# The shared expert's down products moved into the last eight passes of a mixture-of-experts loop

## The reference

```python
    def body(acc, blk):
        tok_b, gate_b, eb = blk
        xb = x_pad[tok_b]
        hb = jax.nn.silu(xb @ w_gate[eb]) * (xb @ w_up[eb])
        yb = hb @ w_down[eb]
        return acc.at[tok_b].add((yb * gate_b[:, None]).astype(acc.dtype)), None
    ...
    shared = (jax.nn.silu(x2 @ w_sh_gate) * (x2 @ w_sh_up)) @ w_sh_down
    return acc[:T] + shared
...
    x = layer_norm(DEEPNORM_ALPHA * x + ffn, ln2_g[i], ln2_b[i])
```

## Time and profile before

| | us |
|---|---|
| median of 3 runs | 1978.24 |
| lowest and highest of them | 1967.44, 1980.79 |
| the profiled execution, whole | 1967.62 |
| its span, first to last instruction | 1965.9 |
| share of the span in which PE is busy | 91% |

### The profile page before, as it was taken

How to read it: one execution, slowest core, us unless ns; L and a number is a source line. 1 busy time by engine, 2 the same in 40 slices (tenths; PEclk the granted TensorE clock), 3 DMA queues, 4 the chain that set the end, 5 groups by cost and what they waited for, 6 DMA issues and landing times. The chain is left out here.

```text
span 1965.9 us, 36214 instructions
## 1 busy us (share of the span) xinstructions
PE 1794.3 (91%) x12636; PEld 1109.1 (56%) x12637; DVE 750.8 (38%) x2168; ACT 384.9 (20%) x882; POOL 354.9 (18%) x450
## 2 busy tenths in 40 slices
PE   9999989889999888879999979999889999997877
PEld 7888444456666555543444438855456666664442
DVE  4222754723332322224255553415623333332225
ACT  2112650111111111102255243211011111110001
POOL 8442000011111111110012712200111111111110
PEclk9999999999999999999999989899999999999999
DMA  6220215599999999999122220015899999999997
GB/s 223 80 84 23 97 59 237 210 397 421 421 421 422 422 422 421 422 421 361 57 65 76 65 42 3 29 60 245 327 408 415 422 421 421 420 421 421 422 415 309
DMA packets 144184, 541.80 MB, mean 276 GB/s; under 512 B 31030, under 2 KB 68498, under 8 KB 94302
## 3 DMA queue, kind: packets, MB, share of 16 engines
q1 hardware_dynamic: 122782, 490.20, 62.2%
q0 software_dynamic: 21312, 50.37, 6.6%
HBM read 521.58 MB, written 46.14 MB: 289 GB/s over the span
## 5 line engine op out<-in xcount | busy, mean ns | idle before, releaser
L718 PE MATMUL bank<-W,XT 128*64 128x256 f32 x2880 | 324.7, 381 | 33.6 <-DMA W<-in_w_exp_up_dram 17.7
L718 PEld LDWEIGHTS bank<-W,XT 128*64 128x64 f32 x2880 | 233.4, 137 | 135.1 <-DMA W<-in_w_exp_gate_dram 26.0
L755 PE MATMUL bank<-W,ht 128*64 128x512 f32 x720 | 166.1, 602 | 13.4 <-DMA W<-in_w_exp_down_dram 8.1
L2237 PE MATMUL bank<-XT,room 128*128 128x512 f32 x352 | 158.9, 606 | 0.0
L729 DVE TENSOR_TENSOR sig<-sig,bank 128x256 f32<-128x256 f32 x72 | 30.3, 421 | 263.7 <-ACT sig L725 263.7
L718 PE MATMUL bank<-room,XT 128*64 128x256 f32 x864 | 104.0, 393 | 17.0 <-DMA room<-in_w_exp_gate_dram 8.8
L731 DVE TENSOR_TENSOR h<-sig,bank 128x256 f32<-128x256 f32 x72 | 30.3, 421 | 218.1 <-PE bank L718 218.0
L2237 PEld LDWEIGHTS bank<-XT,room 128*128 128x128 f32 x352 | 66.3, 193 | 82.3 <-issue 82.1
L784 POOL DMA_INDIRECT y_rows<-y,row x36 | 36.6, 1018 | 418.3 <-DVE y L777 418.3
L784 POOL DMA_INDIRECT y_rows<-XT,row x36 | 36.3, 1008 | 414.5 <-DVE XT L777 414.5
L704 ACT ACTIVATE XT<-bank 128x512 f32<-128x512 f32 x74 | 44.2, 597 | 334.5 <-PE bank L696 334.5
(11 more groups left out here) (490 smaller groups left out, 2793.0 us busy)
## 6 DMA issues: line engine op xcount, KB each, us to landing
W<-in_w_exp_gate_dram SPq DMA_DIRECT2D x88, 1024.0 KB, 25.5
W<-in_w_exp_up_dram SPq DMA_DIRECT2D x88, 1024.0 KB, 27.4
W<-in_w_exp_down_dram SPq DMA_DIRECT2D x88, 1024.0 KB, 26.9
room<-in_w_exp_gate_dram SPq DMA_DIRECT2D x40, 1024.0 KB, 24.2
third_high<-in_w_exp_down_dram SPq DMA_DIRECT2D x40, 1024.0 KB, 25.7
W<-y_rows SPq DMA_DIRECT2D x24, 1024.0 KB, 13.4
third_up<-in_w_exp_up_dram SPq DMA_DIRECT2D x20, 1024.0 KB, 27.5
w_shg<-in_w_exp_up_dram SPq DMA_DIRECT2D x20, 1024.0 KB, 24.2
```

Of the source, the lines that this page charges most:

```text
L718: last = pe.matmul((gate, up)[m][64 * a:64 * a + 64, :], xt[s][:, k, 64 * a:64 * a + 64], weights(w, a, m)[:, k * FE:(k + 1) * FE], start= ...
L755: last = pe.matmul(B[5 + half][64 * a:64 * a + 64, :], ht[:, j, 64 * a:64 * a + 64], weights(w, a, 2)[:, at:at + 512], start=(j == 0), sto ...
L2237: last = pe.matmul(main(i)[:], wc[i % WBUFS][:, kb, :], K.XT[:, kb, :], start=(kb == 0), stop=(kb == KD - 1))
```

## The change

- The loop writes the last eight passes out as well, after the hardware loop, and gives each pair of them a tile: pass 28+2t makes the first half (512 columns) of the shared expert's down product of tile t, pass 29+2t the second. The number of turns less four is computed into a second entry of `plan_turns`.
- In such a pass PE makes the product between the gate and the up products (8 instructions of L1002's kind for a whole tile before, so 4 for a half), in the bank (5 or 6) in which the down products of the pass will be made. It waits for that bank to be emptied by the pass before. DVE replaces x by ALPHA x plus the product (`add_shared`) between its two multiplications; the down products wait for that.
- The combination loses `shared_product` and DVE's scaling; the first `row_product` of a tile starts its sum. Before tile 2, PE waits until banks 5 and 6 have been emptied.
- The shared expert's down weights get a buffer of their own (`w_sh_down_kept`, 8 KB a partition) and are loaded by SP ahead of the first refill of the loop, right behind slot 2's first down matrices.
- To make room, there is one result buffer `y` in place of two: `keep_y` of pass n waits until the scatter of pass n-1 has landed. `sig` is gone: the sigmoid is written to `h`, once `h` of the pass before has been transposed. Three tables of the program's start (`upto`, `level`, a scratch) lie in the weights' arena.

```diff
@@ loop @@
             for u in range(2):
                 body(u, u)
-            turns = eng.value_load(K.plan_turns[0:1, 0:1], min_val=PAIRS // 2, max_val=MAX_PASSES // 2)
-            with eng.Fori(1, turns) as turn:
+            looped = eng.value_load(K.plan_turns[0:1, 1:2], min_val=PAIRS // 2 - NT, max_val=MAX_PASSES // 2 - NT)
+            with eng.Fori(1, looped) as turn:
                 for u in range(2):
                     body(turn * 2 + u, u)
+            for i in range(2 * NT):
+                body(looped * 2 + i, i % 2, i // 2)
...
-        def gate_up(pe, s, n, turn, w):
+        def gate_up(pe, s, n, turn, w, tile):
...
                 last.then_inc(done, 1)
+                if m == 0 and tile is not None:
+                    shared_product(pe, n, tile, s)
+
+        def shared_product(pe, n, tile, half):
+            pe.wait_ge(shared.loaded, 16)
+            pe.wait_ge((y_a, y_d)[half], n)
+            for j in range(2):
+                last = pe.matmul(B[5 + half][:], shared.hidden[:, j, tile * P:(tile + 1) * P],
+                                 shared.w[:, j, half * 512:(half + 1) * 512], start=(j == 0), stop=(j == 1))
+            last.then_inc(shared_made, 1)
+
+        def add_shared(dve, tile, half):
+            dve.wait_ge(shared_made, tile * 2 + half + 1)
+            x = K.X[:, tile, half * 512:half * 512 + 512]
+            dve.scalar_tensor_tensor(x, x, ALPHA, B[5 + half][:], ALU.mult, ALU.add).then_inc(shared_added, 1)
 
         def sigmoid(act, n):
-            wait_from(act, hidden_done, n)
+            wait_from(act, h_turned, n)
             act.wait_ge(gate_done, n + 1)
-            act.activation(sig[:], gate, ACT.Sigmoid).then_inc(sigmoid_done, 1)
-
-        def hidden(dve, n, step):
+            act.activation(h[:], gate, ACT.Sigmoid).then_inc(sigmoid_done, 1)
+
+        def hidden(dve, s, n, step, tile):
             dve.wait_ge(sigmoid_done, n + 1)
-            step(dve.tensor_tensor(sig[:], sig[:], gate, ALU.mult))
+            step(dve.tensor_tensor(h[:], h[:], gate, ALU.mult))
+            if tile is not None:
+                add_shared(dve, tile, s)
             dve.wait_ge(gate_up_done, n + 1)
-            dve.tensor_tensor(h[:], sig[:], up, ALU.mult).then_inc(hidden_done, 1)
+            dve.tensor_tensor(h[:], h[:], up, ALU.mult).then_inc(hidden_done, 1)
...
-        def down(pe, n, turn, w):
+        def down(pe, s, n, turn, w, tile):
+            if tile is not None:
+                pe.wait_ge(shared_added, tile * 2 + s + 1)
...
         def keep_y(eng, s, n, half):
-            wait_from(eng, stored[s], through(n - 2, s))
+            wait_from(eng, stored[1 - s], through(n - 1, 1 - s))
             eng.wait_ge(down_done, 2 * n + 1 + half)
-            dst = y[s][:, half * 512:half * 512 + 512]
+            dst = y[:, half * 512:half * 512 + 512]
@@ SP of expert_loop, ahead of the refills @@
+                shared.load_down(sp, sh_down[:])
                 turns, left = divmod(PAIRS - WSLOTS, WSLOTS)
@@ Combination @@
     def load_early(self, sp):
-        self.shared.load_down(sp, self.down_room)
         self.ln.load(sp)
...
-    def products(self, pe):
-        pe.wait_ge(self.shared.loaded, 16)
+    def products(self, pe, y_a, y_d, passes):
         for t in range(2):
-            self.shared_product(pe, t)
             self.row_product(pe, t, 0)
             self.row_product(pe, t, 1)
-        pe.wait_ge(self.scaled, 1)
         self.row_product(pe, 0, 2)
         self.row_product(pe, 1, 2)
-        self.shared_product(pe, 2)
-        self.row_product(pe, 2, 0)
-        self.row_product(pe, 2, 1)
-        self.row_product(pe, 2, 2)
-        self.shared_product(pe, 3)
+        for y_kept in (y_a, y_d):
+            pe.wait_ge(y_kept, 1)
+            pe.wait_ge(y_kept, passes)
+        for q in range(ROW_PAIRS):
+            self.row_product(pe, 2, q)
         self.turn(pe, 0)
...
         for t in range(NT):
-            dve.tensor_scalar_mul(X[:, t, :], X[:, t, :], ALPHA).then_inc(self.scaled, 1)
-        for t in range(NT):
-            dve.wait_ge(self.scaled, t + 1)
             for half in range(2):
```

More of the change, by code:

```diff
@@ L108, in constants, with carve @@
     K.causal = sb("causal", [P, P], BF16)
-    K.upto = sb("upto_f32", [P, P])
+    made_in = K.arena[:, 4 * TOKW // P * T:4 * TOKW // P * T + NMH // 2 * T]
+    at = [0]
+    def carve(n, dt):
+        size = n * mybir.dt.size(dt) // mybir.dt.size(F32)
+        at[0] += size
+        return made_in[:, at[0] - size:at[0]].bitcast(dt)
+    K.upto = carve(P, F32)
     K.ones = sb("ones_f32", [P, P])
@@ L136, in constants @@
     K.plan_end = sb("plan_end", [1, PAIRS], I32)
-    K.plan_turns = sb("plan_turns", [1, 1], I32)
+    K.plan_turns = sb("plan_turns", [1, 2], I32)
     K.plan_expert = sb("plan_expert", [1, E], I32)
-    scratch = sb("iota_scratch", [P, T // 2], I32)
+    scratch = carve(T // 2, I32)
     K.constants_made = scope.enter_context(nc.semaphore("constants_made"))
@@ L603, in expert_loop @@
         xt = [xt_room[:, (2 + s) * D:(3 + s) * D].rearrange("p (k t) -> p k t", k=KD) for s in range(2)]
-        y = [xt_room[:, 0:D], sb("y1", [P, D])[:]]
+        y = xt_room[:, 0:D]
         turned_gates = sb("turned_gates", [P, 2, NT, ROW_PAIRS])
-        sig, h = sb("sig", [P, FE]), sb("h", [P, FE])
+        h = sb("h", [P, FE])
         ht = sb("ht", [P, 2, P])
@@ L623, in expert_loop @@
         gates_turned = sem("gates_turned")
+        shared_made, shared_added = sem("shared_made"), sem("shared_added")
         steps = sem("steps")
@@ L837, in _, with one_pass @@
                 gather(pool, 1, 1)
-                def one_pass(n, u):
+                def one_pass(n, u, tile=None):
                     read = held(pool, 2 * (n + 1))
@@ L864, in from_slot @@
                     def from_slot(w):
-                        gate_up(pe, u, n, turn, w)
+                        gate_up(pe, u, n, turn, w, tile)
                         if isinstance(n, int) and n == 0:
@@ L870, in from_slot @@
                         slot_rows(pe, 1 - u, n + 3)
-                        down(pe, n, turn, w)
+                        down(pe, u, n, turn, w, tile)
                     if early and n == 0:
@@ L901, in _ @@
                 pe.wait_ge(xt_a, held(pe, turns * 2 + 1))
-                ending.products(pe)
+                ending.products(pe, y_a, y_d, held(pe, turns * 2))
             @block.scalar
@@ L927, in _, with one_pass @@
                 start = step.n
-                def one_pass(n, u):
+                def one_pass(n, u, tile=None):
                     step = Chain(dve, steps, start + n * PASS_STEPS)
-                    hidden(dve, n, step)
+                    hidden(dve, u, n, step, tile)
                     keep_xt(dve, 1 - u, n + 1, 1)
@@ L960, in __init__ @@
         self.two = shared.gate[:, KD * FE - HP:KD * FE]
-        self.down_room = room[:, 1, :]
         self.loaded = [[sem(f"rows_{t}_{q}") for q in range(ROW_PAIRS)] for t in range(NT)]
-        self.added, self.two_made, self.diagonals, self.summed, self.scaled, self.gates_kept = (
-            sem(n) for n in ("added", "two_made", "diagonals", "summed", "scaled", "gates_kept"))
+        self.added, self.two_made, self.diagonals, self.summed, self.gates_kept = (
+            sem(n) for n in ("added", "two_made", "diagonals", "summed", "gates_kept"))
         self.ln = LayerNorm(K, scope, f"ln2_{L}", K.in_["ln2_g"][L:L + 1, :], K.in_["ln2_b"][L:L + 1, :],
@@ L996, in load @@
             sp.wait_ge(K.out_stored, 16 * NT)
-    def shared_product(self, pe, t):
-        B, shared = self.K.banks, self.shared
-        for half in range(2):
-            for j in range(2):
-                pe.matmul(B[2 * t + half][:], shared.hidden[:, j, t * P:(t + 1) * P], shared.w[:, j, half * 512:(half + 1) * 512],
-                          start=(j == 0), stop=False)
     def row_product(self, pe, t, q):
@@ L1012, in row_product @@
                                  self.rows[:, t, q, h, half * 512:(half + 1) * 512],
[L1013 removed]
+                                 start=(q == 0), stop=(q == ROW_PAIRS - 1))
             if q == ROW_PAIRS - 1:
                 last.then_inc(self.summed, 1)
[L1017 to L1018 removed]
+    def products(self, pe, y_a, y_d, passes):
         for t in range(2):
[L1020 removed]
             self.row_product(pe, t, 0)
             self.row_product(pe, t, 1)
[L1023 removed]
         self.row_product(pe, 0, 2)
         self.row_product(pe, 1, 2)
[L1026 to L1030 removed]
+        for y_kept in (y_a, y_d):
[3 more added lines that the diff above has]
+            self.row_product(pe, 2, q)
         self.turn(pe, 0)
```

9 lines of the change are left out of this document (5 added, 4 removed).

## The result

The kernel after the change takes 2022.68 us (median of 4 runs, 2017.79 to 2026.91), the kernel before 1973.1 beside it: a ratio of 1.026, with an interval from 1.023 to 1.0295. The forecast of 1981 and its range up to 2003 are both missed, and so is the slower rival (2008).

What follows compares the result with a forecast made beforehand. Weight streaming was taken to bound both expert loops, PE the combinations behind. Ends -10.7, PE's lateness +14.8 and down weights +1.8 made about +6 us on a mean of 1975.5: 1981 us, range 1961 to 2003.

Steps and rivals of the forecast that it cites:

- the slower rival: Last eight passes: every PE jump over two copies stalls 7.0 us; +32 us, 2008 in all; chance 0.15.
- Where the room is: PE in layer 1 idles 3.8 us per late pass, 2.0 after a half tile; layer 0's passes 28 to 30 have none.
- The cheap-jump rival, A: Last eight passes: first jumps are cheap; layer 1 late by 0.2 us; sum -8, 1967 us; chance 0.28.
- Part 3, the jumps: Written-out last eight passes: four first jumps over two copies per layer at 3.7 us each, those over one copy nothing.
- The ledger of lateness: PE's lateness against the weights, pass by pass: 3.1 us after layer 1's loop, 11.7 after layer 0's, together +14.8.
- Part 1, the end: Combination without shared products: -6.5 us in layer 0, -4.2 in layer 1, -10.7 together, row loads then binding.
- Parts 4 and 5: Down weights loaded first cost +1.8 us of DMA, bounds 0 and 5.2; the one result buffer costs nothing.

Runs made afterwards that it cites:

- e1_one_copy: The changed kernel with one copy of PE's code, so no jump, in each of the last eight passes: 1972.05 us, ratio 1.0006.
- e2_unroll_only: The kernel before with only the last eight passes written out after the hardware loop: 2002.1 us, ratio 1.016.
- e4_in_loop: The changed kernel with one hardware loop, nothing written out, half tiles under a branch on the turn: 1972.21 us, ratio 1.001.
- e3_rest_alone: The changed kernel with one hardware loop and shared products back in the combination; down weights first and one result buffer stay: 1970.96 us, ratio 1.001.
- e8_shift_120: The kernel before with 118 never-executed instructions of waits between the layers, shifting PE's layer 1 code: 1974.83 us, ratio 1.0013.
- e6_placed: The kernel before with PE's code shifted by never-executed waits and the odd pass's copies in the even one's order: 1977.79 us, ratio 1.0024.
- e7_one_copy_placed: e1_one_copy with PE's code shifted by never-executed waits and the odd pass's copies in the even one's order: 1964.10 us, ratio 0.9975.
- e9_one_copy_placed2: e7_one_copy_placed with PE's code at newly counted places, both layers laid alike: 1972.69 us, ratio 1.0016.

## Why the prediction was wrong

**Where the room is: right.** Against eight times 12.81 us, the last eight passes had 119.97 - 102.5 = 17.5 us of room in layer 0 and 132.64 - 102.5 = 30.2 in layer 1. With the jumps gone (e1_one_copy) the moved half tiles leave 2.05 and 0.31 us. The cheap-jump rival, A, had said nothing and 0.2; its other 2.3 us were the down weights' load.

**Part 3, the jumps: the step that failed.** "Jumps over one copy I leave at nothing" was read from two that took 0.39 and 0.45 us, both reached after PE had run for a whole pass. Of the 17 dear ones eleven skip one copy: 20.5 us in layer 0 and 20.1 in layer 1. Two of the eleven are the way into pass 33 in each layer, which the forecast took for one jump over two copies where the code asks two questions: 8.2 and 10.0 us. What it left at nothing is then 12.3 us in layer 0 and 10.1 in layer 1. An odd pass that follows a jump is left no time: its own first question comes 1.6 us behind a landing. The second failing is the size: four at 3.7 us per layer, 14.8 with their clock, where the same four ways took 24.5 and 27.2 us of branches. All told it is 36.8 and 37.3 us of branches and 6.7 and 5.9 of clock. (The 3.7 isn't what the stated scaling gives, 8.3 less the difference of the branches: that makes 4.1 and 2.6 of the two cheap jumps and a mean of some 5. In the trace the passes behind these two are 1.2 and 0.0 us longer than 12.81, so 1.0 and 0 were right, and the mean of those four was; it didn't carry over.) The four jumps seen were taken as one population with a mean; by the count they were of two kinds, into the next block and two on, which hangs on the place of the code, and that was not counted. The rule on blocks was quoted, and "taken strictly" it was applied to the jumps over two copies alone.

**The ledger of lateness: right in form.** With the measured terms, layer 0 has 36.8 + 6.7 + 14.5 - 17.5 = 40.5 us of lateness, against 38.9 measured, and layer 1 37.3 + 5.9 + 14.5 - 30.2 = 27.5, against 28.6. That it closes so well is partly luck. A half tile makes a pass that waits for nothing 2.17 us longer (14.98 for 12.81), not 1.81, so eight cost 17.4 us and not 14.5. And a jump starts while PE still works (that of 809.37 us under down products that run from 809.30 to 812.95), so 36.8 us of jumps left PE idle for 32.1. With these two, layer 0 has 38.7 us against 38.9; layer 1, with 30.7 us of idle time and 2.0 us of room unused, has 25.8 against 28.6, and the rest is open. Here a cover was spent twice: the half tiles alone fit under it (e1_one_copy), the jumps alone exceed it by 16 us per layer (e2_unroll_only), and together all that lies beyond the room arrives at the end. In e2_unroll_only's layer 1 the room was 30.2 us too and not all of it served: PE waited 4.0 and 3.2 us for gate and up matrices, and what is lost in the last passes finds nothing to repay it.

**Part 1, the end: right in layer 1, too much in layer 0.** Forecast 6.5 us in layer 0 and 4.2 in layer 1, 10.7 together. Where the stream still ran to the end it was 3.3 and 4.1 (e1_one_copy), 5.0 and 3.7 (e4_in_loop): in layer 0 the row loads slipped, and PE's last row product of e1_one_copy still waits for one at 930 us, where the forecast had the last one land at 927. In the kernel after it was 17.6, since PE's lateness had let the stream run out, so the last scatter landed in 3.05 us and the loads had the DMA to themselves. What it is above e1_one_copy's 7.4 isn't a gain of the change; it is a part of the loop's loss paid back.

**Parts 4 and 5: nothing, as e3_rest_alone shows.** The 1.8 us for the down weights were too much by about that; the single buffer held ACT once in all of e3_rest_alone, for 3.2 us, and the passes are no longer for it.

**What neither forecast nor rivals had.** The change also moves the first jumps of the loops themselves: 11.6 us of them before, 16.6 to 18.2 in e8_shift_120, the kernel after and e1_one_copy. In e1_one_copy ends 7.4 us shorter and last passes 2.4 longer make 5.0 of gain, and its first jumps take 6.6 more. The trace bears this out in layer 1 alone: passes 1 to 27 are 6.7 us longer there for 4.5 us of jumps, in layer 0 they are 1.8 shorter for 2.1 us of jumps. The stretch between the loops, which holds none of the moved work, is 2.3 us longer; from trace to trace it varies by up to 10.5 us (486.6 in e6_placed, 497.1 in e8_shift_120). So that the first jumps hid the move's worth is likely and not shown; e7_one_copy_placed, with 13.0 us of them and 7.7 us faster than before, speaks for it.

## What to carry to other kernels

Before a loop is written out, count the branches that become first ones, over one copy as over many, with their place in the compiled code, price each at the dearest one seen until a run says otherwise, and look at how busy the DMA is where it will stand; if an engine has several copies of a pass, write out only the one that will run. A wait that the trace shows is room for one thing: add up all that an edit puts under it. And when an experiment shows no change, look for what else moved with it: here, a gain of 5 us stood against 6.6 us of jumps elsewhere.

## What the runs showed of the hardware

- A dear first jump of PE costs 1.4 to 6.7 us while weights stream at 420 GB/s, mostly 4 to 6, and 1.5 to 5.3 with half the bytes. With the DMA idle it is 1.12, 1.64 and 1.68 us in the kernel after; with the row loads at 416 GB/s, the weights long over, it is 4.15 again.
- The same instructions in the same order cost 8.6 us more or less by where they lie (e7_one_copy_placed against e9_one_copy_placed2); the 3.0 us of e8_shift_120 are not clear of the noise.
- The same jump at the same place still varies: layer 0's first took 3.36, 3.39, 3.55, 4.17, 5.50 and 5.50 us in six kernels whose PE code is alike up to there (e2, before, e8, e3, e1, after).
- Three dear jumps in a row (out of pass 32 and two into pass 33, together 14.3 us in layer 0 and 16.0 in layer 1) leave PE idle for 12.8 and 14.6 us, and the granted clock of 876 to 893 us in the kernel after is 0.60.

```profile
...
876.00:893.00 17.00, 5.24 (x30) 3.07 (x32) 0.00 (x0) 0.00 (x0) 2.03 (x2) 0.60 0.66 269
...
```
